# Chunked delta rule: one head per step in three streams, against two heads per step in two streams

## The chip, the core and the metric

The kernel runs on one core of a Trainium2 chip. Its time is the device time of one execution in microseconds (us). A core has TensorE (PE, whose weight loads are shown as PEld), VectorE (DVE), ScalarE (ACT), GpSimd (POOL) and SyncE (SP, which issues the transfers). Each of them works through its own instructions in the order in which the program gives them, and waits for the others through semaphores.

## The reference

Two transformer-like blocks on 256 tokens of width 1024, all in float32. The first block mixes tokens with a gated delta rule over 8 heads of 128 columns, in chunks:

```python
# per head; in the kernel a chunk is 128 rows, so 2 chunks per head
decay = exp(where(causal, g[c] - g[s], -inf))
lower = where(strict, (k_beta @ k.T) * decay, 0)
t_inv = triangular_solve(eye + lower, eye, lower=True, unit_diagonal=True)
u  = t_inv @ v_beta;  w = t_inv @ (k_beta * exp(g))
qk = where(causal, (q @ k.T) * decay, 0)
v_new = u - w @ state
o     = q_g @ state + qk @ v_new
state = state * exp(g_last) + k_dec.T @ v_new
```

Around it stand the projections (q, k, v, z, gates, a short convolution branch, `proj`, `wo`), an FFN, then a second block with attention and a gated FFN. All of them are products of the 1024-wide activations with weights that are read once from HBM.

## The kernel before

**Products.** Weights are float32, read in items of 1 MB into three buffers `raw`. A unit is half an item: ACT writes its high part `wh` (fp32r, line 1459), DVE the rest `wl` (line 1851), into five buffers in turn. PE then makes, for each 128-column tile of a unit, 12 matmuls of 128 rows by 256 columns: 8 on line 1094 (high activations with `wh` and `wl`) and 4 on line 1100 (low activations with `wh`). Such a row of 12 matmuls is a *tick* below; a product of 256 columns has 4 ticks. Ticks are counted here from the first product (q of the first two heads). Up to tick 50 come q, k, v (and the small `ab`), to 98 the three of the convolution branch, then gb to 114, z to 130, scout to 146, ga to 162, proj to 178, wo to 194. Beside gb, z and scout DVE also sums one item of the modulation weights per product (`ada`: lines 1747 and 1750, on 128x512).

**The order.** A planner in Python writes one list of events. After each tick it calls `tick()`, which lets every open task add its next event; all engines then walk the same list and take their own part of each event. So an event that falls after tick 40 stands on PE between the matmuls of ticks 40 and 41, whenever its operands come.

**The delta rule.** The task `gdn(h)` carries head `h` through 21 steps. Step `k` adds the event `gdn` (PE's part of it, in `pe_gdn`) and `gdn_out` `k+1` (what ACT, DVE and POOL make of its result, in `act_gdn`, `dve_gdn`, `pool_engine`). Three heads are open at a time, each with its own PSUM bank (5 to 7) and tiles; `beat` makes the steps fall alternately one and two ticks apart. The steps:

- 0: PE spreads the head's decay row over all partitions (lines 1113, 1114: 8 rows by 128 columns of weights, 256 columns moving) and turns `KT` (1116). DVE makes `dec` and `k0`, ACT the exponentials (1360, 1361).
- 1: PE makes k k^T and q k^T (1120, 1122). DVE makes `l2`, `qk`, `xz`, `qg` (1651 to 1660), ACT copies the diagonal 64x64 blocks out (1365).
- 2 to 12: the inverse of the two 64x64 diagonal blocks of each chunk, doubled from 1 to 64 in six levels; `xz` holds both the inverse and its transpose, and PE updates both. Step 2 turns `xz` (1128), odd steps multiply by the level's part of the lower triangle (1139), even ones by the inverse (1147 and 1150). All these are 64x64 matmuls, one in the upper and one in the lower 64 partitions. DVE subtracts (1666), ACT copies (1373), POOL cuts the levels out (2061, 2067).
- 13, 14: the remaining 64x64 block of the 128x128 inverse (1156, 1161).
- 15 to 20: values, state, output, and the sum of squares for the norm (1166 to 1184, all 128x128 or 128x256).

After it `oz` multiplies with z and splits the result for `proj`; before `proj` starts, all tasks are drained.

**Fixed waits between the parts.** The values of heads 2j and 2j+1 need the task `conv_qkv`: ACT's block of SiLU, squares and high parts (from line 1540 to 1549, with a load of the SiLU table in front), then a transpose on PE (1298) and two sums (1305, 1307), then exponentials again, for which `ln_exp` loads the other table.

Of the kernel before, what the change touches and what calls it, by code (L numbers as in the profile page):

```python
# [11 lines left out]
T = 256  # L12
# [4 lines left out]
APART = 1  # L17
LN_EXP = 6
LATER = 6
STREAMS = 3  # L20
WARM = 9
LEVELS = [1, 2, 4, 8, 16, 32]
# [14 lines left out]
for _name, _n in (("eye", 128), ("ones", 128), ("eps", 1), ("lnq", 1), ("cmask", 128), ("eye64", 64), ("lev", 6 * 64)):  # L37
    CST[_name] = _at
    _at += _n
# [4 lines left out]
def constants():  # L44
# [5 lines left out]
    s, t = i[:, None] % 64, i[None, 0:64]  # L50
    c[:, CST["eye64"]:CST["eye64"] + 64] = s == t
    for n, m in enumerate(LEVELS):
        lev = (s // (2 * m) == t // (2 * m)) & (s // m % 2 == 0) & (t // m % 2 == 1)
        c[:, CST["lev"] + 64 * n:CST["lev"] + 64 * (n + 1)] = np.where(lev, -1.0 if n == 0 else 1.0, 0.0)
# [54 lines left out]
class Counting:  # L109
# [14 lines left out]
    def transpose(self, out, in_, eye):  # L124
        return self
# [59 lines left out]
def _program(nc, a, out, ctx):  # L185
# [3 lines left out]
    def signal(name, step=1):  # L189
# [50 lines left out]
    GH = sb("GH", [8, T], F32R, where=mixer)  # L240
    GL = sb("GL", [8, T], F32R, where=mixer)
    eyeR = sb("eyeR", [8, 8], F32R, where=mixer)
# [6 lines left out]
    streams = [dict(  # L249
        dec=sb(f"dec{i}", [128, 2, 128], where=mixer), l2=sb(f"l2{i}", [128, 2, 128], where=mixer),  # L250
        qk=sb(f"qk{i}", [128, 2, 128], where=mixer), lc=sb(f"lc{i}", [128, 2, 64], where=mixer),
        d0=sb(f"d0{i}", [128, 2, 64], where=mixer), d1=sb(f"d1{i}", [128, 2, 64], where=mixer),
        xz=sb(f"xz{i}", [128, 2, 2, 64], where=mixer), y=sb(f"y{i}", [128, 2, 64], where=mixer),
        inv=sb(f"inv{i}", [128, 2, 128], where=mixer), v=sb(f"v{i}", [128, 2, 128], where=mixer),
        s1=sb(f"s1{i}", [128, 128], where=mixer),
        k0=sb(f"k0{i}", [128, 128], where=mixer), qg=sb(f"qg{i}", [128, 128], where=mixer),
        sh=sb(f"sh{i}", [128, T], F32R, where=mixer), sl=sb(f"sl{i}", [128, T], F32R, where=mixer),
        bank=psum[8 - STREAMS + i]) for i in range(STREAMS)]
# [42 lines left out]
    lev = cst[:, CST["lev"]:CST["lev"] + 384].rearrange("p (a b) -> p a b", a=6)  # L301
    eye64 = cst[:, CST["eye64"]:CST["eye64"] + 64]
    lo, hi = slice(0, 64), slice(64, 128)
    c0, c1 = slice(0, 128), slice(128, 256)
# [88 lines left out]
    main, misc = Ring(range(3)), Ring((3, 4))  # L393
# [201 lines left out]
    def conv_qkv(p):  # L595
# [33 lines left out]
        tasks.append(gdn(2 * j))  # L629
        tasks.append(gdn(2 * j + 1))  # L630
# [16 lines left out]
    before_head, before_attend = {}, {}  # L647

    def beat(k):

        yield
        while ticks[0] % 3 != (1 if k in (0, 2, 4, 6, 8, 10, 12, 14, 17) else 0):
            yield

    def gdn(h):
        while not open_streams:
            yield
        st, before_head[h] = open_streams.pop(0)
        while ("decays", 4, 0) not in made:
            yield  # L660
        if before_head[h] is None:
            for _ in range(APART * st):
                yield from beat(0)
        yield from beat(0)
        for k in range(21):
            emit("gdn", h, k, st)
            emit("gdn_out", h, k + 1, st)
            if k == 1:
                yield from beat(k)
            yield from beat(k + 1)  # L670
        open_streams.append((st, h))
        while ("z", "ready", h // 2) not in made or ("m", 3) not in made:
            yield
        while h > 1 and ("oz", h - 2, 0) not in made:
            yield
        emit("oz", h, 0)
        yield
        emit("oz", h, 1)
# [96 lines left out]
    def after(p):  # L775
# [5 lines left out]
        elif kind in ("z", "gb", "ga"):  # L781
            if kind == "ga":
                until(("gdn", 2 * j, 17), ("gdn", 2 * j + 1, 17))
# [70 lines left out]
    def operands_of(p, unit):  # L854
# [5 lines left out]
        if src == "o":  # L860
            return [("oz", kt, 1) for kt in kts]
# [1335 lines left out]
```

## Time and profile before

| | |
|---|---|
| three runs, us | 924.0, 913.3, 921.08 |
| median | 921.08 |
| the profiled execution | 913.96 |
| its span in the trace | 912.2 |
| PE busy | 881.9 us, 97% |
| DVE busy | 669.5 us, 73% |
| ACT busy | 508.0 us, 56% |
| POOL busy | 72.1 us, 8% |
| mean granted clock of TensorE | 0.998 |
| DMA | 177.31 MB, mean 194 GB/s |

Of the execution's own time, 1.8 us lie outside the span.
### The profile page before, as it was taken

The page shows a single profiled execution, that of the slowest core. Times are in us where ns is not written, and L with a number is a line of the kernel's source. Part 1 is how long each engine was busy: PE and PEld are TensorE (multiplying, and loading weights), DVE is VectorE, ACT ScalarE, POOL GpSimd, SP SyncE. Part 2 cuts the span into 40 slices and gives each one's busy share as a digit, 9 for nine tenths or more (in the row PEclk, how much of TensorE's full clock was granted, in tenths as well). Part 3 has the DMA queues.
Part 4 walks back from the last instruction along what each step waited for, and adds up shares of the span by engine and source line. Part 5 has one row for each costly group of instructions (what it writes and reads, how often), then busy time and mean ns, then how long its engine had stood idle before and what let it go on. Part 6 is the DMA issues. An engine that isn't in the chain of part 4 may idle for free.

```text
span 912.2 us, 18654 instructions
## 1 busy us (share of the span) xinstructions
PE 881.9 (97%) x8020; PEld 840.6 (92%) x8020; DVE 669.5 (73%) x1132; ACT 508.0 (56%) x822; POOL 72.1 (8%) x91
## 2 busy tenths in 40 slices
PE   5897999999999999999999999999999999999997
PEld 2797899999898989999999999999888999999997
DVE  3877877566979687677888885578666778888653
ACT  2489668453344637655354444556665567666442
POOL 0101122021001101020000000220000200000011
PEclk9999999999999999999999999999999999999999
DMA  8754232332776664465998889635332436555631
GB/s 337 277 190 170 93 137 97 139 139 97 248 259 230 233 231 164 167 216 182 269 338 292 286 291 259 227 121 189 137 141 93 182 139 210 207 185 175 251 130 47
DMA packets 27681, 177.31 MB, mean 194 GB/s; under 512 B 2864, under 2 KB 5680, under 8 KB 7504
## 3 DMA queue, kind: packets, MB, share of 16 engines
q1 hardware_dynamic: 27600, 176.13, 55.1%
q8 instruction: 63, 1.03, 0.5%
q14 instruction: 18, 0.15, 0.0%
HBM read 174.29 MB, written 1.84 MB: 193 GB/s over the span
## 4 chain that ended last, share of the span: by engine, by line
PE 76%; DVE 10%; ACT 7%; DMA 4%; issue 1%; POOL 1%; DVEq 0%; SPq 0%; ACTq 0%
PE ps L1094 42%; PE ps L1100 20%; DVE wl L1851 3%; DMA raw<-in_w_fi_dram 2%; ACT wh L1459 2%; DVE acc L1750 2%; PE ps L1092 2%; PE ps L1139 1%; PE ps L1147 1%; PE ps L1233 1%; PE ps L1150 1%; PE ps L1098 1%; DMA raw<-in_ada_dram 1%; DMA raw<-in_w_sc_dram 1%; DVE KT L1733 1%
## 5 line engine op out<-in xcount | busy, mean ns | idle before, releaser
L1851 DVE TENSOR_TENSOR wl<-raw,wh 128x1024 fp32r<-128x1024 f32 x265 | 322.0, 1235 | 76.2 <-ACT wh L1459 75.5
L1094 PE MATMUL ps<-HH,wh 128*128 128x256 f32 x1480 | 367.4, 285 | 0.7 <-ACT HH L1433 0.2
L1094 PE MATMUL ps<-HH,wl 128*128 128x256 f32 x1480 | 357.4, 278 | 0.0
L1459 ACT ACTIVATE wh<-raw 128x1024 fp32r<-128x1024 f32 x265 | 273.4, 1042 | 140.3 <-PE ps L1100 109.2
L1094 PEld LDWEIGHTS ps<-HH,wh 128*128 128x128 f32 x1480 | 279.2, 189 | 8.2 <-issue 2.9
L1094 PEld LDWEIGHTS ps<-HH,wl 128*128 128x128 f32 x1480 | 278.9, 188 | 0.4
L1100 PE MATMUL ps<-HL,wh 128*128 128x256 f32 x1480 | 226.6, 278 | 0.3 <-DVE HL L1796 0.3
L1100 PEld LDWEIGHTS ps<-HL,wh 128*128 128x128 f32 x1480 | 195.2, 188 | 0.6 <-DVE HL L1796 0.5
L1094 PE MATMUL ps<-FH,wh 128*128 128x256 f32 x352 | 84.5, 276 | 0.0
L1094 PE MATMUL ps<-FH,wl 128*128 128x256 f32 x352 | 84.5, 276 | 0.0
L1750 DVE SCALAR_TENSOR_TENSOR acc<-raw,silc,acc 128x512 f32<-128x512 f32 x101 | 76.3, 756 | 8.0 <-DMA raw<-in_ada_dram 5.0
L1094 PEld LDWEIGHTS ps<-FH,wl 128*128 128x128 f32 x352 | 66.1, 188 | 0.0
L1094 PEld LDWEIGHTS ps<-FH,wh 128*128 128x128 f32 x352 | 66.1, 188 | 0.0
L1733 DVE SCALAR_TENSOR_TENSOR tmp<-ps,vec,tmp 128x255 f32<-128x255 f32 (+2 forms) x112 | 46.1, 476 | 22.4 <-ACT tmp L1527 21.1
L1100 PE MATMUL ps<-FL,wh 128*128 128x256 f32 x352 | 55.5, 276 | 0.0
L2091 POOL TENSOR_TENSOR sq<-sq 128x256 f32<-128x256 f32 x16 | 14.8, 930 | 510.9 <-ACT sq L1501 510.7
L1100 PEld LDWEIGHTS ps<-FL,wh 128*128 128x128 f32 x352 | 47.0, 188 | 0.0
L1623 ACT ACTIVATE FH<-tmp 128x512 fp32r<-128x512 f32 x22 | 13.9, 633 | 57.7 <-DVE tmp L2019 30.1
L1094 PE MATMUL ps<-YH,wh 128*128 128x256 f32 x128 | 32.0, 286 | 0.0
L1094 PE MATMUL ps<-YH,wl 128*128 128x256 f32 x128 | 30.9, 277 | 0.0
L1094 PEld LDWEIGHTS ps<-YH,wh 128*128 128x128 f32 x128 | 24.1, 188 | 0.5
L1527 ACT ACTIVATE tmp<-ps,vec 128x256 f32<-128x256 f32 x44 | 22.1, 552 | 3.6 <-PE ps L1100 3.6
(273 smaller groups left out, 1088.2 us busy)
## 6 DMA issues: line engine op xcount, KB each, us to landing
raw<-in_ada_dram SPq DMA_DIRECT2D x32, 1024.0 KB, 5.4
raw<-in_w_fi_dram SPq DMA_DIRECT2D x22, 1024.0 KB, 5.0
raw<-in_w_up_dram SPq DMA_DIRECT2D x22, 1024.0 KB, 4.8
raw<-in_w_rest_dram SPq DMA_DIRECT2D x20, 1024.0 KB, 4.7
raw<-in_w_in_dram SPq DMA_DIRECT2D x16, 1024.0 KB, 4.8
raw<-in_w_qkv_dram SPq DMA_DIRECT2D x12, 1024.0 KB, 4.8
raw<-in_w_o_dram SPq DMA_DIRECT2D x8, 1024.0 KB, 4.9
raw<-in_w_fo_dram SPq DMA_DIRECT2D x8, 1024.0 KB, 4.9
```

The lines of the kernel that those rows point to most:

```text
L1092: e.matmul(o, x_hi[:, k0 + k, 128 * t:128 * t + 128], w[:, k, :], start=first and n + k == 0, **MM)
L1094: e.matmul(o, w[:, k, 128 * t:128 * t + 128], x_hi[:, k0 + k, :], start=first and n + k == 0, **MM)
L1098: ins = e.matmul(o, x_lo[:, k0 + k, 128 * t:128 * t + 128], wh[:, k, :], start=False, **MM)
L1100: ins = e.matmul(o, wh[:, k, 128 * t:128 * t + 128], x_lo[:, k0 + k, :], start=False, **MM)
L1139: ins = e.matmul(bank[g, 64 * c:64 * c + 64], S[f"d{n % 2}"][g, c, :], xz[g, 0, c, :], start=True, **MM)
L1459: e.activation(whl[u % HALF][0][:, 0:n], raw[i % RAW][:, c:c + n], ACT.Copy).then_inc(*a_hi.up(u))
L1527: e.activation(tmps[m][:, T * t:T * t + T], b[:, T * t:T * t + T], ACT.Identity, scale=v("conv2", 88 + ft), bias=v("conv2_b", ft)).then_in ...
L1623: e.activation(flat(dst, j), tmps[m][:, :], ACT.Copy).then_inc(*a_ev.up("hi", src, j))
L1733: e.scalar_tensor_tensor(out=cv, in0=b[:, T * t:T * t + T - s], scalar=tap, in1=cv, op0=ALU.mult, op1=ALU.add).then_inc(*v_ev.up("conv", n ...
L1750: ins = e.scalar_tensor_tensor(out=acc_, in0=w, scalar=c, in1=acc_, op0=ALU.mult, op1=ALU.add)
L1851: e.tensor_tensor(wl[:, 0:n], raw[i % RAW][:, c:c + n], wh[:, 0:n].bitcast(F32), ALU.subtract).then_inc(*v_lo.up(u))
L2091: e.tensor_tensor(sqs[s][:, 0:T], sqs[s][:, 0:T], sqs[s][:, T:2 * T], ALU.add).then_inc(*g_norm.up(*(("sum", n, j) if j else ("part", n, 0))))
```

## The change

Two heads (a *pair*, 2j and 2j+1) go through every step together, on tiles of four parts (two heads by two chunks) and one PSUM bank. Two pairs are open at a time instead of three heads, in banks 5 and 6, and bank 7 joins the small `misc` ring until proj. Steps fall on even ticks, two ticks apart, and four ticks apart after steps 0, 1, 10 and 19; so the steps of both streams fall on the same ticks.

The diagonal is inverted in 32x32 blocks with five levels instead of six; only `z` is updated by PE, and its transpose `x` comes from a DVE block transpose after each update. Steps 11 and 12 then put two 32 blocks together to 64 (both the block and its transpose), steps 13 and 14 two 64 to 128. POOL makes all levels of the lower triangle in one instruction `d` (it was five of them), also `qg` (it was on DVE), and spreads x and z into block diagonal `x64` and `inv`. `GH`, `GL` and `eyeR` get 128 rows, of which 120 are zero, so the decay matmuls of step 0 use the whole array. The transpose of `KT` for `k0` moves from step 0 to step 15, and the scaling of it from DVE to ACT. `qk` is made one step later (step 3).

```diff
-STREAMS = 3
+STREAMS = 2
+GRID = 2
+HEAVY = (0, 1, 10, 19)
-LEVELS = [1, 2, 4, 8, 16, 32]
+LEVELS = [1, 2, 4, 8, 16]
...
     def beat(k):
 
+        for _ in range(2 if k in HEAVY else 1):
+            yield
+            while ticks[0] % GRID:
+                yield
...
         elif k == 1:
-            a_gdn.wait_ge(e, "eg", h)
-            for c in range(2):
-                e.matmul(bank[:, cs[c]], KT[:, h, cs[c]], KT[:, h, cs[c]], start=True, **MM)
-            for c in range(2):
-                ins = e.matmul(bank[:, 256 + 128 * c:384 + 128 * c], KT[:, h, cs[c]], QT[:, h, cs[c]], start=True, **MM)
-            ins.then_inc(*p_gdn.up(h, 1))
+            v_misc.wait_ge(e, "l2", j, 1)
+            a_gdn.wait_ge(e, "eg", j)
+            for i, h in heads_of:
+                for c in range(2):
+                    ins = e.matmul(b4[:, 2 * i + c, :], KT[:, h, cs[c]], KT[:, h, cs[c]], start=True, **MM)
+            ins.then_inc(*p_gdn.up(j, 1))
...
-            for c in range(2):
-                for g in (lo, hi):
-                    ins = e.matmul(bank[g, 64 * c:64 * c + 64], S[f"d{n % 2}"][g, c, :], xz[g, 0, c, :], start=True,
-                                   **MM)
-            ins.then_inc(*p_gdn.up(h, k))
-        elif k < 13:
+            v_gdn.wait_ge(e, "x", j, n - 1)
+            for i in range(4):
+                for q in quarter:
+                    ins = e.matmul(bank[q, 32 * i:32 * i + 32], S["d"][q, n - 1, i, :], x[q, i, :], start=True, **MM)
+            ins.then_inc(*p_gdn.up(j, k))
+        elif k < 11:
             n = (k - 2) // 2
-            a_gdn.wait_ge(e, "y", h, n)
-            for c in range(2):
-                for g in (lo, hi) if n < 5 else (lo,):
-                    e.matmul(bank[g, 64 * c:64 * c + 64], xz[g, 1, c, :], S["y"][g, c, :], start=True, **MM)
-            for c in range(2):
-                for g in (lo, hi):
-                    ins = e.matmul(bank[g, 128 + 64 * c:192 + 64 * c], S["y"][g, c, :], xz[g, 1, c, :], start=True,
-                                   **MM)
-            ins.then_inc(*p_gdn.up(h, k))
+            a_gdn.wait_ge(e, "y", j, n)
+            for i in range(4):
+                for q in quarter:
+                    ins = e.matmul(bank[q, 128 + 32 * i:160 + 32 * i], y[q, i, :], z[q, i, :], start=True, **MM)
+            ins.then_inc(*p_gdn.up(j, k))
...
-        elif 5 <= k < 13 and k % 2:
+        elif 5 <= k < 12 and k % 2:
             n = (k - 3) // 2
-            p_gdn.wait_ge(e, h, k - 1)
-            xz4 = xz[:, :, :, :].rearrange("p a b c -> p (a b c)")
-            e.tensor_tensor(xz4, xz4, b[:, 0:T], ALU.subtract).then_inc(*v_gdn.up("xz", h, n))
+            p_gdn.wait_ge(e, j, k - 1)
+            e.tensor_tensor(z[:, :, :], z[:, :, :], by_four(S, 128), ALU.subtract).then_inc(*v_gdn.up("z", j, n))
+            v_gdn.wait_ge(e, "z", j, n)
+            e.transpose(S["x"][:, :, :].rearrange("p a b -> p (a b)"), z[:, :, :].rearrange("p a b -> p (a b)")).then_inc(
+                *v_gdn.up("x", j, n))
...
                 if k == 2:
-                    a_gdn.wait_ge(e, "lc", h)
-                    for n in (1, 2):
-                        e.tensor_tensor(S[f"d{n % 2}"][:, :, :], S["lc"][:, :, :],
-                                        lev[:, n:n + 1, :].broadcast_to([128, 2, 64]), ALU.mult).then_inc(
-                            *g_gdn.up("d", h, n))
-                elif k in (4, 6, 8):
-                    n = (k - 2) // 2
-                    p_gdn.wait_ge(e, h, k - 1)
-                    e.tensor_tensor(S[f"d{n % 2}"][:, :, :], S["lc"][:, :, :],
-                                    lev[:, n + 2:n + 3, :].broadcast_to([128, 2, 64]), ALU.mult).then_inc(
-                        *g_gdn.up("d", h, n + 2))
+                    a_gdn.wait_ge(e, "lc", j)
+                    e.tensor_tensor(S["d"][:, :, :, :], S["lc"][:, None, :, :].broadcast_to([128, 4, 4, 32]),
+                                    lev[:, 1:5, None, :].broadcast_to([128, 4, 4, 32]), ALU.mult).then_inc(
+                        *g_gdn.up("d", j))
```

On PE, before, in the inverse of the first two heads: step 4 of both heads (banks 5 and 6) after the last low matmuls of a tick and ahead of the next tick.

```order
L1100 MATMUL ps1<-HL,wh4 128x256 x4
L1147 MATMUL ps5<-y0,xz0 64x64 x4
L1150 MATMUL ps5<-xz0,y0 64x64 x4
L1147 MATMUL ps6<-y1,xz1 64x64 x4
L1150 MATMUL ps6<-xz1,y1 64x64 x4
L1094 MATMUL ps1<-HH,wh0 128x256
```

On PE, in the change, at the corresponding place: a step of the inverse of two pairs, thus of four heads.

```order
L1120 MATMUL ps0<-HL,wh3 128x256 x4
L1163 MATMUL ps5<-x0,d0 32x32 x16
L1163 MATMUL ps6<-x1,d1 32x32 x16
L1114 MATMUL ps0<-HH,wh4 128x256
L1114 MATMUL ps0<-HH,wl4 128x256
```

Where each even step had one half-array pair of matmuls for the inverse and one for its transpose, the change has 16 matmuls of 32x32 per pair of heads, and the transposes are on DVE.

On ACT, before, around the SiLU block of heads 2 and 3: the exponentials of head 0 (lines 1360, 1361) stand behind the block.

```order
L1533 ACTIVATE tmp<-ps,vec 128x256 x2
L1459 ACTIVATE wh<-raw 128x1024
L1540 ACT_TABLE_LOAD
L1540 ACTIVATE QT<-QT 128x512
L1540 ACTIVATE KT<-KT 128x512
L1540 ACTIVATE tmp<-tmp 128x512
L1544 ACTIVATE sq<-QT 128x512
L1544 ACTIVATE sq<-KT 128x512
L1549 ACTIVATE sqh<-sq 128x512 x2
L1324 ACT_TABLE_LOAD
L1360 ACTIVATE qg<-ps 128x128
L1361 ACTIVATE dec<-dec 128x256
```

In the change, the same place: the exponentials of the first pair (lines 1413, 1415) stand ahead of the block, and the load of the other table stands further behind.

```order
L1597 ACTIVATE tmp<-ps,vec 128x256 x2
L1413 ACTIVATE dec<-dec 128x512
L1415 ACTIVATE qg<-ps 128x128 x2
L1523 ACTIVATE wh<-raw 128x1024
L1604 ACT_TABLE_LOAD
L1604 ACTIVATE QT<-QT 128x512
L1604 ACTIVATE KT<-KT 128x512
L1604 ACTIVATE tmp<-tmp 128x512
L1608 ACTIVATE sq<-QT 128x512
L1608 ACTIVATE sq<-KT 128x512
L1613 ACTIVATE sqh<-sq 128x512 x2
L1523 ACTIVATE wh<-raw 128x1024
```

The block itself is the same; what moved is the pair of exponentials that PE's step 1 waits for. Counted over the whole program, TensorE leaves full-size matmuls for a part of the array and comes back 65 times in the 64x64 steps before (and 8 times for lines 1113 and 1114), and 36 times in the change. The steps of the inverse have 528 matmuls of 64x64 before; in the change they have 592 of 32x32 (lines 1163 to 1185 of it) and 32 of 64x64. The full-size matmuls of the steps are the same in number, but for step 20, where 16 of 256 columns become 8 of 512.

## Rows read from the trace of the kernel before

**Rows 1.** The page: busy time and share of the engines.

```profile
PE 881.9 (97%) x8020; PEld 840.6 (92%) x8020; DVE 669.5 (73%) x1132; ACT 508.0 (56%) x822; POOL 72.1 (8%) x91
```

**Rows 2.** Busy time by stage: length, PE, PEld, DVE, ACT, POOL, clock, DMA.

```profile
81.80:366.81 285.01, 276.20 (x2927) 260.14 (x2927) 216.95 (x402) 159.90 (x291) 37.41 (x54) 0.99 0.49 174
81.80:136.61 54.81, 49.93 (x539) 46.57 (x540) 41.72 (x87) 39.41 (x72) 10.79 (x16) 0.97 0.36 132
136.61:238.93 102.32, 102.15 (x1133) 95.57 (x1132) 72.56 (x143) 54.06 (x103) 14.48 (x21) 1.00 0.36 127
238.93:342.32 103.39, 99.63 (x1048) 93.71 (x1047) 83.82 (x143) 49.10 (x86) 8.74 (x15) 1.00 0.69 244
...
478.44:540.70 62.26, 62.26 (x546) 62.26 (x545) 52.07 (x63) 29.29 (x34) 0.00 (x0) 1.00 0.84 289
```

**Rows 3.** What PE waited for from 80 to 370 us: us, times, longest.

```profile
PE ps L1120 <- ACT qg L1360: 6.6, 4, 4.0
PE ps L1156 <- DVE inv L1672: 1.3, 1, 1.3
PE ps L1172 <- ACT s L1379: 0.7, 1, 0.7
```

**Rows 4.** PE in order of time around two visits to the 64x64 steps.

```profile
109.75 0.63 PE L1100 MATMUL ps<-HL,wh 128*128 128x256 f32 x4
110.31 0.68 PE L1139 MATMUL ps<-xz,d 64*64 64x64 f32 x16
110.92 0.38 PE L1094 MATMUL ps<-HH,wh 128*128 128x256 f32 x1
...
111.97 0.63 PE L1100 MATMUL ps<-HL,wh 128*128 128x256 f32 x4
...
113.61 0.38 PE L1094 MATMUL ps<-HH,wh 128*128 128x256 f32 x1
```

**Rows 5.** PE in order of time, 64x64 matmuls in one half only.

```profile
144.12 0.44 PE L1156 MATMUL ps<-xz,l 64*64 64x64 f32 x4
144.47 0.45 PE L1139 MATMUL ps<-xz,d 64*64 64x64 f32 x8
```

**Rows 6.** The chain that ended last: start, us, what.

```profile
721.34 2.01 PE ps L1213 x18
```

**Rows 7.** PE in order of time around the decay matmuls.

```profile
92.24 0.62 PE L1100 MATMUL ps<-HL,wh 128*128 128x256 f32 x4
...
92.79 0.38 PE L1113 MATMUL ps<-GH,eyeR 8*128 8x256 f32 x1
...
93.21 0.33 PE L1116 MATMUL ps<-cst,KT 128*128 128x128 f32 x1
```

**Rows 8.** All engines in order of time, at the end of a SiLU block.

```profile
87.28 1.28 ACT L1324 ACT_TABLE_LOAD   x1
88.57 0.28 ACT L1360 ACTIVATE qg<-ps 128x128 f32<-128x128 f32 x1
...
88.90 1.23 PE L1120 MATMUL ps<-KT 128*128 128x128 f32 x4 [4.03 <-ACT qg L1360]
```

**Rows 9.** POOL's groups from 88 to 415 us, by shape.

```profile
L2067 POOL TENSOR_TENSOR d<-lc,cst 128x128 f32<-128x128 f32 x24 | 13.2, 561 | 70.5 <-PE ps L1139 70.5
...
L2080 POOL TENSOR_TENSOR sql<-sq,sqh 128x512 fp32r<-128x512 f32 x6 | 8.1, 1376 | 30.1 <-ACT sqh L1549 30.1
```

**Rows 10.** DVE's groups from 88 to 415 us, by shape.

```profile
L1851 DVE TENSOR_TENSOR wl<-raw,wh 128x1024 fp32r<-128x1024 f32 x83 | 103.2, 1254 | 13.7 <-ACT wh L1459 13.5
L1750 DVE SCALAR_TENSOR_TENSOR acc<-raw,silc,acc 128x512 f32<-128x512 f32 x42 | 31.7, 754 | 1.3
L1666 DVE TENSOR_TENSOR xz<-xz,ps 128x256 f32<-128x256 f32 x32 | 13.0, 417 | 14.5 <-PE ps L1150 14.2
...
L1660 DVE TENSOR_TENSOR xz<-xz,cst 128x128 f32<-128x128 f32 x8 | 4.0, 498 | 0.0
...
L1655 DVE TENSOR_TENSOR xz<-lc,cst 128x128 f32<-128x128 f32 x8 | 2.3, 292 | 3.0 <-ACT lc L1365 3.0
```

More of the change, by code:

```diff
@@ L36 @@
 _at = 0
-for _name, _n in (("eye", 128), ("ones", 128), ("eps", 1), ("lnq", 1), ("cmask", 128), ("eye64", 64), ("lev", 6 * 64)):
+for _name, _n in (("eye", 128), ("ones", 128), ("eps", 1), ("lnq", 1), ("cmask", 128), ("eye32", 32), ("own", 4), ("lev", 5 * 32)):
     CST[_name] = _at
@@ L122, in matmul, with transpose @@
         return self
-    def transpose(self, out, in_, eye):
+    def transpose(self, out, in_, eye=None):
         return self
@@ L248, in _program, with stream, one @@
     dt_y, dt_abs, dt_g = (M[0:8, n, :] for n in range(3))
[L249 to L258, printed above, removed]
+    def stream(i):
+        S = {}
+        def one(name, shape, dt=F32, where=mixer):
+            S[name] = sb(f"{name}{i}", shape, dt, where=where)
+        one("dec", [128, 4, 128])
+        with ExitStack() as turn:
+            one("l2", [128, 4, 128], where=turn)
+            one("v", [128, 2, 2, 128], where=turn)
+        one("sh", [128, 512], F32R)
+        one("sl", [128, 512], F32R)
+        one("qk", [128, 4, 128])
+        one("lc", [128, 4, 32])
+        one("d", [128, 4, 4, 32])
+        one("z", [128, 4, 32])
+        one("x", [128, 4, 32])
+        one("y", [128, 4, 32])
+        one("x64", [128, 4, 64])
+        one("y64", [128, 4, 64])
+        one("inv", [128, 4, 128])
+        one("s1", [128, 2, 128])
+        one("k0", [128, 2, 128])
+        one("qg", [128, 2, 128])
+        S["bank"] = psum[5 + i]
+        return S
+    streams = [stream(i) for i in range(STREAMS)]
     mixer.close()
@@ L953, in _program @@
             drain()
+            misc.order[:] = [b for b in misc.order if b[0] != 7]
         key = p["kind"], p["j"]
@@ L1163, in pe_gdn @@
         elif k == 15:
-            v_gdn.wait_ge(e, "inv", h)
+            v_gdn.wait_ge(e, "inv", j)
             a_misc.wait_ge(e, "vturn", j)
-            e.matmul(bank[:, c0], S["inv"][:, 0, :], V[:, h, 0, :], start=True, **MM).then_inc(*p_gdn.up(h, k))
+            for i, h in heads_of:
+                e.matmul(bank[:, 128 * i:128 * i + 128], S["inv"][:, 2 * i, :], V[:, h, 0, :], start=True, **MM)
+            for i, h in heads_of:
+                ins = e.transpose(bank[:, 256 + 128 * i:384 + 128 * i], KT[:, h, c0], eye)
@@ L1167, in pe_gdn @@
+            ins.then_inc(*p_gdn.up(j, k))
         elif k == 16:
-            v_gdn.wait_ge(e, "v0", h)
-            e.matmul(bank[:, c0], S["k0"][:, :], S["v"][:, 0, :], start=True, **MM).then_inc(*p_gdn.up(h, k))
+            a_gdn.wait_ge(e, "k0", j)
+            for i in range(2):
+                ins = e.matmul(bank[:, 128 * i:128 * i + 128], S["k0"][:, i, :], S["v"][:, i, 0, :], start=True, **MM)
+            ins.then_inc(*p_gdn.up(j, k))
         elif k == 17:
-            a_gdn.wait_ge(e, "s1", h)
@@ new lines, in pe_gdn @@
+            for i in range(2):
+                ins = e.matmul(bank[:, 128 * i:128 * i + 128], S["inv"][:, 2 * i + 1, :], S["k0"][:, i, :], start=True,
+                               **MM)
+            ins.then_inc(*p_gdn.up(j, k))
+        elif k == 19:
+            v_gdn.wait_ge(e, "v1", j)
+            g_gdn.wait_ge(e, "qg", j)
+            for i in range(2):
+                e.matmul(b4[:, 2 * i, :], S["v"][:, i, 0, :], S["qk"][:, 2 * i, :], start=True, **MM)
+                e.matmul(b4[:, 2 * i + 1, :], S["s1"][:, i, :], S["qg"][:, i, :], start=True, **MM)
+                ins = e.matmul(b4[:, 2 * i + 1, :], S["v"][:, i, 1, :], S["qk"][:, 2 * i + 1, :], start=False, **MM)
+            ins.then_inc(*p_gdn.up(j, k))
@@ L1636, in dve_gdn @@
         if k == 1:
[L1637 removed]
+            p_gdn.wait_ge(e, j, 0)
             v_misc.wait_ge(e, "neg")
             d_masks.wait_ge(e, "masks")
[L1640 to L1644 removed]
```

390 lines of the change are left out of this document (221 added, 169 removed).

## The prediction

> **What bounds the kernel now.** I read the page first: PE is busy for 97% of the span, DVE 73%, ACT 56% [rows 1]. Then the stages. The delta rule runs between ticks 28 and 162, from 81.80 to 366.81 us, and in each part of that PE has least room; DVE comes nearest from 238.93 to 342.32, with 83.8 of 103.4 us [rows 2]. Then PE's waits: from 80 to 370 us it waited visibly for 8.6 us, 6.6 of them for ACT's exponentials ahead of step 1 [rows 3]. So what PE has to do there sets the time, and a microsecond less on PE is a microsecond less in the end while the others keep up.
>
> What does the delta rule cost on PE? A stage without it gives the price of a tick: 44 ticks in 62.26 us [rows 2], 1.415 us each, 0.118 per matmul. The 134 ticks of the section need 189.6 us at that price; it took 285.0. So 95.4 us are spent on the steps, on their waits and on a few other matmuls.
>
> **The change part by part.**
>
> *Visits to a part of the array.* In [rows 4] the four low matmuls start at 109.75 and would be over at 110.22; the next tick starts at 110.92. So 8 small matmuls (16 records) cost 0.70 us. At the next visit the same reckoning gives 113.61 - 112.44 = 1.17 us for 32 records. The difference, 0.47 us for 16 records, is 0.0294 per record; what remains, 0.23 us, is the price of going there and back. With 65 visits that is 15.0 us before. The change has 36, thus 8.3, and four inner switches from 32 to 64, for which I take 0.1 each: 8.7.
>
> *The small matmuls before.* The 528 matmuls leave 1056 records. 96 of them, those of line 1147 in level five and all of 1156 and 1161, stand in one half of the array alone. There four records take 0.35 us with part of the entry in it [rows 5]; I take 0.059 each, twice 0.0294, so that two halves run at the same time and one alone does not gain. 960 x 0.0294 + 96 x 0.059 = 33.9 us. With the visits: 48.9.
>
> *The small matmuls after.* No row shows 32x32. The 32 matmuls of 64x64 go from one half to the other: 64 records x 0.059 = 3.8 us. The 592 of 32x32 leave 1184 records. 512 of the matmuls stand in four quarters, 32 in two, 48 in three (their tiles differ in rows or columns), so they can form 320 sets of records that run together. What is the price of a set? A full record of 128 columns takes 2.01 / 18 = 0.112 us [rows 6], one of 64 takes 0.059. On the line through these two, 32 columns come to 0.032; if narrowing gives nothing more, it stays 0.059. I take 0.032, because halving from 128 to 64 gave nearly half: 10.2 us, with 18.9 as the upper bound. If the quarters don't run together at all, 1184 records cost 37 us at 0.032 and 70 at 0.059; these are ends of the range and rivals below. My sum after is 8.7 + 3.8 + 10.2 = 22.7, **26.2 us less**.
>
> The two halves that run together in [rows 4] have different rows of the array and write the same PSUM bank, at different partitions. The Trainium skill (TensorEngine Tiling (Array Packing), Gotcha 1: PSUM Pressure) says that different row tiles cannot access the same PSUM bank at the same time; this trace does not agree for two tiles, and by that rule the quarters, which share a bank as well, would run one by one. The same page (Instruction Overhead) gives each matmul some 60 cycles of overhead and warns against tiling a dimension that is small already; by that rule a set would stay near the 64-column price, and the sum would be that of the upper bound, 18.9 us. No row here shows a matmul this narrow.
>
> *Decay matmuls.* With 8 rows they too leave the full array: from 92.71 (four low matmuls after 92.24) to 93.21, 0.50 us per head [rows 7]. With 128 rows they cost two plain ones, 0.24. Eight heads: **2.1 us less**. Their price with zero rows can't be below the plain one, and at 0.50 nothing would be gained.
>
> *Full-size matmuls of the steps.* Their number stays; 16 moving 256 columns become 8 moving 512. Zero. `KT`'s transpose moves from step 0 to 15: zero on PE, and step 0 no longer waits for `l2` through it.
>
> *Waits.* Before: 8.6 us visible, and in 81.80 to 136.61 the mean granted clock was 0.97 [rows 2]: after the wait of 4.0 us at 88.9 [rows 8] matmuls ran for a while at the lower level, 1.2 GHz; 3% of 54.8 is 1.6 us. Together 10.2. The first wait comes from ACT: the exponentials stand behind the SiLU block and a table load, and are ready at 88.9. In the change they stand ahead of the block, and step 1 finds them there. What is late next is the sum of line 1307, which needs squares from the same block and a POOL operation of 1.38 us [rows 9]: I take 1.3 us there, since PE arrives about 4 us earlier and had no wait before. The other waits, 4.6 us in all, arise where steps are one tick apart, 1.4 us; two ticks, and four for the long steps, take most of them. Against this the answers get longer: ACT and DVE take all four parts at a time, and each update of z is followed by a transpose on DVE. No row shows one; it lies between a plain 128x128 operation from SBUF at 0.29 and a slow one at 0.50 [rows 10], I take 0.35, near the plain one. Subtract and transpose then are 0.7 us against 0.42 before, well inside two ticks of 2.8 unless the queue in front is long. POOL's `d` has four times the elements of an operation of 0.56 us [rows 9], so 1.4 to 2.2 us, with six ticks to do it in. I leave 6 us of waits: **4.2 us less**.
>
> *DVE.* Its work falls: by the shapes of [rows 10] it is a quarter less for the steps (fewer and wider instructions, `qg` and the scaling of `k0` gone, 20 transposes new). In the stage from 238.93 the groups of the steps add up to about 20 of DVE's 83.8 us, so it comes to about 79. PE's part beyond its 48 ticks there is 103.4 - 67.9 = 35.5 us; shrunk like the whole, by 32.5 of 95.4, it leaves a stage of 91.3 us. DVE would be at 87%, against 84% in the stage at 478.44, where PE never waits for it [rows 2]. That is near enough to allow **2.5 us of new waits**. DMA moved 244 GB/s there and would have to move 277; the stage at 478.44 moved 289 without making PE wait.
>
> Sum: 26.2 + 2.1 + 4.2 - 2.5 = 30.0 us. The profiled execution took 913.96 us, so **884 us** on its terms. It is at the low end of the three runs shown (913.3 to 924.0, median 921.08). A new kernel's median should lie a few microseconds above such a low run too; I take 3 of these 7 and say 887.
>
> **The rivals.**
>
> *A, late answers.* PE's steps come at fixed ticks, and DVE works its queue in order. Where an item of the modulation sums (four operations of 0.75 us) and a `wl` (1.2) stand [rows 10] ahead of z's update, the answer takes some 5 us where the ticks leave 2.8 to 3.5. For it: twelve such items fall between ticks 98 and 146, DVE at 87%. Against: PE waited there for DVE only once in this way, 1.3 us [rows 3]. Eight waits of 1.5 us instead of the 2.5 in my sum: 887 + 9.5, some 896.
>
> *B, narrow gains nothing.* A set stays at 0.059: 8.7 us more, 896.
>
> *C, quarters in turn.* The 32x32 matmuls run one by one: 27 us more at 0.032, thus 914 (no change); at 0.059, 59 more, thus 946. This is the case on the other side: against the median of 921 it decides at (34 + 10.2) / 1184 = 0.037 us per record run alone. For it: quarters are finer than anything shown, with 48 in which two share rows. Against: the halves do run together [rows 4].
>
> *D, given back.* The section gets shorter and a later stage waits for its weights or for DVE. The stages behind it keep their own work, and DMA's mean is 194 of the 289 GB/s shown. If half were lost, 902.
>
> **How the numbers follow.** My case 0.58, A 0.16, B 0.10, C 0.11 (half of it each way), D 0.05. The range has to leave out no more than 2 in 10: from 876 (waits nearly gone, low runs) to 905, which takes in A, B, D and leaves out C. One per cent, 9 us, is about what a measurement of this kernel can tell from no change. Faster by over that means below 912: my case, A, B, D, and a little of C: 0.89. Within it: 0.06. Slower by over it: 0.05.
>
> **What would show it.** Records of the 32x32 steps should start in fours within some 0.03 us, 16 matmuls costing 0.25 us and a visit 0.23 more. Ticks 28 to 162 should take about 255 us instead of 285; the ticks from 98 to 146 some 91 to 94 instead of 103. Step 1 of the first pair should find its exponentials ready, and PE should wait a little at a sum of squares. Starts of 32x32 records that are all 0.03 or 0.06 apart show C; sets 0.06 apart show B; PE waiting for DVE's x in the stage with the modulation sums shows A. The prediction is wrong if ACT, which now answers with wider copies behind the same blocks, makes every step late, or if DVE's transpose costs several times 0.35.

## The result, and the profile after

| | before | changed |
|---|---|---|
| runs beside each other, us | 913.3 to 924.0 (4) | 885.61 to 893.53 (4) |
| median, us | 921.98 | 890.86 |
| ratio | | 0.9673, 95% interval 0.9593 to 0.9753 |
| the profiled execution, us | 913.96 | 893.02 |
| ticks 28 to 162, us | 285.0 | 257.2 |

The kernel is 3.3% faster. The predicted 887 us lies 4 us under the median. On two other chips (below) the change had medians of 889.02 and 886.26 us, ratios 0.9715 and 0.9675.

First the page of the changed kernel, busy time and share of the engines, beside [rows 1]:

```profile
PE 859.3 (96%) x8204; PEld 826.7 (93%) x8204; DVE 659.5 (74%) x1079; ACT 501.3 (56%) x770; POOL 67.2 (8%) x63
```

PE is still the bound and has 22.6 us less busy time. Then its stages, to be laid beside [rows 2] (length, PE, PEld, DVE, ACT, POOL, clock, DMA): ticks 28 to 162 in one, then ticks 28 to 50, 50 to 98, 98 to 146, and everything behind tick 162.

```profile
80.57:337.74 257.17, 246.46 (x3111) 237.76 (x3110) 207.86 (x351) 153.48 (x240) 32.50 (x26) 0.99 0.54 193
80.57:133.29 52.72, 44.64 (x638) 42.19 (x636) 41.74 (x85) 40.17 (x71) 8.94 (x8) 0.97 0.37 127
133.29:228.65 95.36, 92.72 (x1257) 88.86 (x1249) 71.64 (x132) 53.10 (x89) 14.87 (x12) 0.99 0.41 143
228.65:315.12 86.47, 86.47 (x1038) 84.09 (x1033) 75.89 (x115) 47.74 (x66) 8.69 (x6) 0.99 0.76 273
...
337.74:891.20 553.46, 545.03 (x4626) 534.00 (x4624) 394.04 (x627) 298.50 (x451) 27.89 (x27) 1.00 0.56 194
```

All of the gain is in the section of the delta rule: 2.1, 7.0 and 16.9 us in the three stages shown. The last row is what an unchanged program took behind it, 553.5 us; the kernel before took 545.4 there (366.81 to 912.20). That is why the profiled executions differ by 20.9 us and the medians by 31. Two more profiles of the same kernel, below, settle it.

PE's waits in the section, beside [rows 3] (us in total, times, longest):

```profile
PE ps L1170 <- ACT y L1424: 4.0, 1, 4.0
PE ps L1163 <- DVE x L1734: 2.6, 1, 2.6
PE ps L1163 <- DVE qk L1728: 1.6, 1, 1.6
PE ps L1351 <- ACT tmp L1604: 1.4, 1, 1.4
PE ps L1360 <- POOL sql L2165: 0.6, 1, 0.6
PE ps L1147 <- ACT qg L1415: 0.5, 1, 0.5
```

They come to 10.7 us; before they were 8.6. None of the old ones is left at its size, and each new one is somewhere else.

PE in order of time around one visit to the 32x32 steps, beside [rows 4]:

```profile
106.34 0.62 PE L1120 MATMUL ps<-HL,wh 128*128 128x256 f32 x4
...
106.88 0.45 PE L1163 MATMUL ps<-x,d 32*32 32x32 f32 x32
...
107.27 0.39 PE L1114 MATMUL ps<-HH,wh 128*128 128x256 f32 x1
107.49 0.28 PE L1114 MATMUL ps<-HH,wl 128*128 128x256 f32 x1
```

The four low matmuls would be over at 106.81 (106.34 + 4 x 0.118), the next tick starts at 107.27: 16 matmuls, for two heads, cost 0.46 us with the way there and back. Before, 8 matmuls for one head cost 0.70 [rows 4]. In the single records four start 7 ns apart, one for each quarter of the array, and the next four 31.6 ns after the first: 8 such sets are 0.25 us, and the visit is the other 0.21. The last line matters too: the second matmul of the tick starts 0.22 us behind the first, where product matmuls otherwise start 0.12 us apart. That belongs to the price of a visit as well, and comes back in the part on the prediction.

### The profile page after: what moved, and what is told of

It is laid out like the page before. It is cut to its first block, busy times and chain, and to the rows that moved or that the text cites. A ratio compares the mean times of both kernels' runs of the same rounds, so it can differ in the third digit from the quotient of the medians.

```text
span 891.2 us, 18860 instructions
## 1 busy us (share of the span) xinstructions
PE 859.3 (96%) x8204; PEld 826.7 (93%) x8204; DVE 659.5 (74%) x1079; ACT 501.3 (56%) x770; POOL 67.2 (8%) x63
## 3 DMA queue, kind: packets, MB, share of 16 engines
HBM read 174.16 MB, written 1.84 MB: 197 GB/s over the span
## 4 chain that ended last, share of the span: by engine, by line
PE 82%; DVE 9%; ACT 6%; DMA 1%; issue 1%; POOL 1%; DVEq 0%; SPq 0%; ACTq 0%
PE ps L1114 47%; PE ps L1120 23%; DVE wl L1930 2%; PE ps L1112 2%; ACT wh L1523 1%; PE ps L1286 1%; DVE acc L1829 1%; PE ps L1118 1%; DMA raw<-in_ada_dram 1%; DVE KT L1812 1%; PE ps L1306 1%; PE ps L1163 1%; PE ps L1170 1%; DMA raw<-in_w_in_dram 1%; PE ps L1260 0%
## 5 line engine op out<-in xcount | busy, mean ns | idle before, releaser
L1114 PE MATMUL ps<-HH,wl 128*128 128x256 f32 x1480 | 361.2, 280 | 0.0
```

The costliest lines, as they stand in the source:

```text
L1114: e.matmul(o, w[:, k, 128 * t:128 * t + 128], x_hi[:, k0 + k, :], start=first and n + k == 0, **MM)
```

## The experiments

Four kernels ran on a first chip (kernel before: median 916.06), four on a second (915.90), four on a third (915.55). Ratios are to the kernel before on the same chip. Where a step's wait falls ahead of tick 28 in one kernel and behind it in another, I compare ticks 0 to 162.

### The quarters in turn

```diff
-            for i in range(4):
-                for q in quarter:
+            for q in quarter:
+                for i in range(4):
```

(in the odd and the even steps 3 to 10)

> The change, with the loops of steps 3 to 10 turned round: all four matmuls of one quarter, then the next quarter, so that neighbours share their tile and can't run together except where the quarter changes. Same matmuls, same results. If the gain of the 32x32 steps rests on four quarters running together, 1024 records cost 0.032 us each instead of 0.008: 16 matmuls in some 0.9 to 1.0 us instead of 0.27, in all about 22 us more than the change. If PE's time there is set by issue or by the visit (rival), the price stays and the time is that of the change within 3 us.

Measured: 896.43 us (892.5 to 898.84), ratio 0.977 (0.9721 to 0.9819). The same place as above in its trace:

```profile
109.32 0.62 PE L1120 MATMUL ps<-HL,wh 128*128 128x256 f32 x4
109.87 0.89 PE L1163 MATMUL ps<-x,d 32*32 32x32 f32 x32
110.69 0.39 PE L1114 MATMUL ps<-HH,wh 128*128 128x256 f32 x1
```

Now 32 records take 110.69 - 109.79 = 0.90 us, 0.44 more, thus 14 us in 32 such groups. I had expected 22, from 0.032 us for each record run alone; 0.90 less the visit's 0.21 is 0.022 each. The section grew by 9.9 (267.1 us), since the wait for y fell from 4.0 to 1.9 and that for x from 2.6 to 1.8. So the order of issue matters: the quarters side by side are what makes the narrow matmuls cheap. The starts in such a group are mostly 26 to 32 ns apart, with pairs 5 ns apart among them, so some records of neighbouring quarters still ran together.

### The narrow matmuls twice

```diff
-            for i in range(4):
+            for i in (0, 1, 2, 3) * 2:
                 for q in quarter:
```

> Each 32x32 matmul of the steps 3 to 10 is issued twice, with the same result: 1024 more records in 256 sets of four, and not one visit, eviction or step more. Theory 1: the steps lie on the path and cost what they issue, 256 x 31.6 ns = 8.1 us, so section ticks 28 to 162 at 265 us. Theory 2: the time of the section is set by the answers of VectorE and ScalarE, which have the rest of the beat to come; then the matmuls are partly covered where PE waits (10.7 us of waits), and the section grows by 4 us or less. Theory 3: the 7 ns spacing is of the records alone and TensorE works longer than they show; then the next product starts later, and the section grows by more than 12 us.

Measured: 901.28 us (899.7 to 904.65), ratio 0.9844 (0.982 to 0.9867); section 270.1 us, 12.7 more than the unaltered change on that chip (257.5). The waits of its section:

```profile
PE ps L1170 <- ACT y L1424: 3.1, 1, 3.1
PE ps L1170 <- issue: 2.9, 2, 1.8
PE ps L1163 <- DVE x L1734: 2.0, 1, 2.0
```

Theory 1 has the right mechanism, but sizes it too low: all groups that stand between product matmuls took 9.6 us more than in the unaltered change, idle time left out (63.8 against 54.2), where it has 8.1. A set of four takes 37 ns on the mean of the section, not the 31.6 of the group shown. The waits that PE already had covered only 1.5 us of the extra work (y 4.0 to 3.1, x 2.6 to 2.0), so theory 2 falls: these matmuls are on the path. So does theory 3, although its total fits: the next product starts 0.12 us behind the last narrow record in both kernels. The rest is new: three pauses "issue", 3.5 us (the 2.9 above and one of 0.6 on L1163), in the middle of a run of narrow records, where PE waits for nothing that the profile shows, and a fourth of 0.5 us among the low matmuls just ahead of such a run:

```profile
240.81 1.30 PE L1170 MATMUL ps<-z,y 32*32 32x32 f32 x126
243.94 0.21 PE L1170 MATMUL ps<-z,y 32*32 32x32 f32 x2 [1.84 <-issue]
```

128 records had to be issued in about a microsecond there, and two of them came 1.84 us late. Instructions are fetched by DMA (the page has a queue of kind instruction), and from 242 to 244 us the transfers of weights took 97% of the engines; but the pause of 0.56 us at 131.8 falls where no transfer ran. That PE ran out of instructions is my guess; what held them up was not tried. With the matmuls once, the section of the change shows no such pause. 9.6 - 1.5 + 4.0 is 12.1 of the 12.7 us.

### The streams on odd and even ticks

The second pair's steps go on odd ticks, the first's on even ones, so the two streams no longer share a visit.

> The change, with the second stream on odd ticks instead of the common even ones. TensorE leaves the full array 48 times instead of 36. If a visit costs 0.23 us, 2.8 us more on TensorE in ticks 28 to 162; the waits may fall or rise by some 2 us with the other places. If the common beat matters by more than the visits (rival: it also bunches the answers, or spares them), the time moves by over 5 us either way.

Measured: 893.11 us (892.36 to 895.78), ratio 0.9743 (0.9701 to 0.9786); section 265.1, 7.9 more than the change. TensorE has 84 groups of step matmuls in its order instead of 53. The 12 additional visits at 0.23 would be 2.8 us; measured without idle time, all groups between product matmuls took 1.3 us more (55.8 against 54.5), and the slow first distances behind them 2.2 more, as they are 86 instead of 62. The waits account for the rest:

```profile
PE ps L1170 <- ACT y L1424: 6.5, 1, 6.5
PE ps L1163 <- DVE qk L1728: 2.0, 2, 1.7
```

Its waits over 0.4 us, with x 1.9, v 1.6 and four smaller, come to 15.3 instead of 10.7, and there are 10.2 us at half clock instead of 6.8 (below). So the common beat is worth something, about 3.5 us by its groups and the distances behind them; how much of the remaining 4.4 us is the beat's and how much the accident of where the y copy meets the SiLU block isn't told apart.

### The decay matmuls with 8 rows

`GH`, `GL` and `eyeR` get their 8 rows back.

> The change, with GH, GL and eyeR back at 8 rows, so that the decay matmuls of step 0 use 8 rows of the array. By the rows of before each head's two matmuls cost 0.50 us instead of 0.24: 2.1 us more in all, which a timing hardly tells and the starts in the trace do. If the zero rows cost as much as they save (rival), the starts stand as far apart as with 128 rows.

One run, 885.41 us; section 257.0 us. TensorE around the first pair's decay matmuls:

```profile
77.77 0.38 PE L1139 MATMUL ps<-GH,eyeR 8*128 8x256 f32 x1
77.99 0.28 PE L1140 MATMUL ps<-GL,eyeR 8*128 8x256 f32 x1
...
78.44 0.39 PE L1114 MATMUL ps<-HH,wh 128*128 128x256 f32 x1
```

and with 128 rows in the change:

```profile
77.39 0.28 PE L1139 MATMUL ps<-GH,eyeR 128*128 128x256 f32 x1
...
77.85 0.28 PE L1114 MATMUL ps<-HH,wh 128*128 128x256 f32 x1
```

From the first to the product behind, four matmuls take 0.67 us instead of 0.46, and the way in another 0.1: 0.3 us for a pair, 1.2 in all. Two heads back to back pay it once, so of the 2.1 us that I gave to the zero rows the pairing had already taken 0.9. (The distance behind, 78.44 to 78.66, is 0.22 us here and 0.12 with 128 rows, another 0.1 for a pair.) The section doesn't show even the 1.2, and the first of the four pairs lies ahead of it. What hides the rest is the clock: PE waited 2.6 us for x here as in the change (until 228.8 us), but no half clock followed. The row of one microsecond behind that wait, here and in the second profile of the change (the last columns are POOL, the clock, the DMA share and GB/s):

```profile
230.00:231.00 1.00, 1.00 (x10) 1.00 (x10) 1.00 (x2) 0.20 (x1) 0.00 (x0) 1.00 0.87 352
```

```profile
230.00:231.00 1.00, 1.00 (x7) 1.00 (x6) 1.00 (x2) 0.00 (x0) 0.00 (x0) 0.50 0.98 418
```

That is worth some 1.6 us to this run (below), more than the edit costs it in the section.

### No long beats, and the change beside it

```diff
-HEAVY = (0, 1, 10, 19)
+HEAVY = ()
```

> The change, with no steps of four ticks: every step two ticks after the last. Step 1 then has 2.8 us in which DVE makes four dec, ACT three exponentials; step 2 after 1 and 11 after 10, 20 after 19 likewise. My theory: TensorE waits at these steps, about 1 to 2 us at each of four places in four pairs, in part at once for both streams: 8 to 15 us more than the change. Rival: the delta rule ends 8 ticks per pair earlier and nothing waits for it, while the answers are quick enough: the same time within 3 us.

Measured: 883.86 us (881.94 to 887.07), ratio 0.9635 (0.958 to 0.969). My theory of 8 to 15 us more fell. The change itself ran again on the second chip:

> The changed kernel once more, unaltered, as the measure for the others of this set: its profiled run had a tail (ticks 392 to the end) 7 us longer than the kernel before, at an unchanged program there. Theory: that is noise of one execution, so this profile has the tail of the kernel before (185.5 us from tick 392 on, it was 192.3) and a section of 257 us for ticks 28 to 162 again; time 884 to 893. Rival: the change itself lengthens the tail, and it is again near 192 us.

Measured: 889.02 us (885.27 to 895.05), ratio 0.9715 (0.9684 to 0.9746). Section 257.5 us, and 185.5 us from tick 392 on, as in the kernel before. The longer tail of the first profile was that execution's and not the change's. And on the third chip:

> The changed kernel unaltered, as the measure on this chip: section ticks 0 to 162 at 300.5 to 301 us, time 884 to 893 us.

Measured: 886.26 us (885.16 to 893.38), ratio 0.9675 (0.9635 to 0.9714); ticks 0 to 162 in 300.46 us. Beside it:

> HEAVY empty a second time, now beside the unaltered change on one chip. Theory: the steps that PE visits together fall from 53 groups to 48 and the largest wait (y, 3.97 us in tick 42) falls to 1.45 because the pairs meet the SiLU block at another step; against that stands a wait of 3.26 us for qg in tick 28. Ticks 0 to 162 took 296.5 us against 300.5, so the median lies 3 to 6 us under the unaltered change. Rival: the first look was a lucky execution, and the two are within 1.5 us.

Measured: 881.51 us (881.14 to 883.72), ratio 0.9615 (0.958 to 0.9651), 4.7 us under the change on the same chip. This is the fastest kernel of the study. Ticks 0 to 162 of both, the change first:

```profile
37.92:338.38 300.46, 288.37 (x3460) 278.48 (x3461) 243.61 (x413) 191.24 (x300) 37.33 (x30) 0.99 0.53 192
```

```profile
38.08:335.03 296.95, 286.48 (x3460) 276.28 (x3461) 244.14 (x413) 189.77 (x299) 37.92 (x30) 0.99 0.54 194
```

and what PE waited for without long beats:

```profile
PE ps L1147 <- ACT qg L1415: 3.4, 1, 3.4
PE ps L1163 <- DVE qk L1728: 2.0, 1, 2.0
PE ps L1170 <- ACT y L1424: 1.4, 1, 1.4
PE ps L1163 <- DVE x L1734: 1.2, 2, 0.6
PE ps L1222 <- DVE k L1758: 0.9, 1, 0.9
```

The long beats were there to give step 1 time, and they do: without them it waits 3.4 us for qg, with them 0.5. But they lay the y copy behind the SiLU block (4.0 us against 1.4) and x in tick 98 behind the modulation sums (2.6 against 0.6). Waits from tick 27 on come to 9.1 us against 10.7, one stretch at half clock falls away (1.6 us), and six groups fewer between the products save 0.5 us of slow distances behind them. That is 3.7 us where 3.5 were measured. The visits themselves save nothing: what falls away are groups of full-size matmuls, both kernels go to a part of the array 36 times, and without idle time the groups take 56.7 us with long beats and 56.8 without.

### A long beat at step 0 alone

> HEAVY = (0,): only the step of the decays is followed by a long beat. Theory 1: the first exponentials get one tick more, so the wait for qg at step 1 (3.26 us without long beats) is under 1 us and the rest stays as without long beats: ticks 0 to 162 at 294 us. Theory 2: the later steps move by one tick, meet the SiLU block and the convolutions elsewhere, and a wait for qk, y or x of 3 to 5 us comes in its place, as in both kernels with the SiLU block one tick later: 299 us or more.

Measured: 885.93 us (883.7 to 886.74), ratio 0.9655 (0.9622 to 0.9688); ticks 0 to 162 in 298.3 us. Its waits:

```profile
PE ps L1163 <- DVE qk L1728: 4.6, 1, 4.6
...
PE ps L1147 <- ACT qg L1415: 0.5, 1, 0.5
```

The wait for qg is gone as planned, and one of 4.6 us for qk stands in its place. Theory 2.

### The SiLU block one tick later

One more `yield` in `conv_qkv` ahead of the event `silu`, which puts the block behind the y copy that waited for it.

> The largest wait left, 3.97 us in tick 42, is for ScalarE's copy y of one pair, which stands in its queue behind the SiLU block of the next pair. Here that block is put into the queue one tick later. Theory 1: the copy goes ahead, the wait is gone and about 4 us with it (section ticks 28 to 162 at 253, time ratio to the unaltered change 0.995). Theory 2: what the block feeds (the SiLU, the sums of squares and the l2 scales of the next pair) is needed just as urgently, so the wait reappears a few ticks later and the time stays.

Measured: 894.94 us (893.8 to 896.43), ratio 0.977 (0.9752 to 0.9789), ticks 0 to 162 in 307.3 us. Theory 1 fell.

```profile
PE ps L1164 <- DVE qk L1729: 5.4, 2, 5.1
PE ps L1352 <- ACT tmp L1605: 4.2, 2, 2.4
```

Every wait of the block's own results grew (tmp 1.4 to 4.2), and PE still waits for y, 3.1 us. The same edit without long beats:

> The edit of the SiLU block together with no long beats (HEAVY empty), which alone gave a section of 249.9 us. Theory 1: the two gains are of different waits and add, section near 246 us. Theory 2: without long beats the pairs already meet the SiLU block at another step (the wait there was 1.45 us), so this adds at most 1 us to the kernel without long beats.

Measured: 894.6 us (891.29 to 901.14), ratio 0.9772 (0.9744 to 0.9799), ticks 0 to 162 in 307.6 us: worse than the kernel without long beats by 11 us, which neither theory held. The largest waits are qg 5.2 in three, qk 5.1, y 2.7, tmp 2.6.

### GpSimd's d behind the transpose

```diff
                     a_gdn.wait_ge(e, "lc", j)
+                    v_gdn.wait_ge(e, "x", j, 0)
                     e.tensor_tensor(S["d"][:, :, :, :], ...
```

> GpSimd makes d only when VectorE has made the first x of the pair. Theory: VectorE's addition z<-z,cst (128x128) takes 1.08 us because GpSimd's d runs beside it, so now it takes 0.30 to 0.50 us, with the same work in both engines; d is ready 1.3 us later, still ahead of step 3 (at least one tick, 1.4 us, behind step 2), so ticks 0 to 162 within 1 us of 300.5, with the wait for qk in tick 36 (1.57 us) shorter by up to 0.7 us if VectorE's queue is what makes it late. Rival: the addition is slow by itself (operand shapes), then it takes 1.08 us again.

Measured: 885.51 us (885.34 to 886.48), ratio 0.9656 (0.9616 to 0.9696), ticks 0 to 162 in 300.5 us. In the change, and then with the edit:

```profile
92.78 1.21 POOL L2140 TENSOR_TENSOR d<-lc,cst 128x512 f32<-128x512 f32 x1 [0.84 <-ACT lc L1420]
93.06 1.08 DVE L1721 TENSOR_TENSOR z<-z,cst 128x128 f32<-128x128 f32 x1
```

```profile
93.64 0.29 DVE L1721 TENSOR_TENSOR z<-z,cst 128x128 f32<-128x128 f32 x1
93.97 0.31 DVE L1724 STREAM_TRANSPOSE x<-z 128x128 f32<-128x128 f32 x1
...
94.43 1.10 POOL L2141 TENSOR_TENSOR d<-lc,cst 128x512 f32<-128x512 f32 x1 [1.90 <-DVE x L1724]
```

The addition goes from 1.08 to 0.29 us in all four pairs. It was GpSimd beside it that slowed it. (`d` itself took 1.20 to 1.22 us in the change and takes 1.10 to 1.94 here.) The wait for qk fell from 1.6 to 0.8 us as well. Yet the section is as long as before: PE came to the y copy 0.87 us earlier, waited there 4.0 us all the same, and the half clock lasted 6.8 us instead of 3.4 (from 112.7 to 119.5, of which 5.5 us lie behind the wait), which took it back.

## Why the prediction was right

**The bound** was read rightly: a microsecond less of PE's own work was a microsecond less in the end. Twice the narrow matmuls cost the whole of their issue time and more.

**Visits and small matmuls, -26.2, and decay matmuls, -2.1.** To check them without the waits, I added up in both traces the time from the start of a product's matmul to the start of the next one wherever step matmuls stand between, less 0.118, and took off the idle time in it: 79.2 us before, 50.3 after, 28.9 less, where I had 28.3. The parts: a visit 0.21 (taken 0.23); a set of four quarters 31.6 ns in the group shown and 37 on the mean of the section (taken 0.032, on a line through 128 and 64 columns); a 64x64 record alone 58 ns (0.059); the decay matmuls of a pair 0.46 us from 77.39 to 77.85, so 0.23 per head (0.24). These held as far as they go. But [rows 4] stop at the first matmul behind the visit. The next line of that view is:

```profile
111.14 0.28 PE L1094 MATMUL ps<-HH,wl 128*128 128x256 f32 x1
```

It starts 0.22 us behind the one of 110.92, not 0.12. At full clock such a slow distance stands behind 78 of the 85 groups between the products before and 50 of 60 after; the others end in full-size fp32r matmuls. What all these first distances take over the usual 0.115 us is 7.87 us before and 4.93 after: a gain of 2.9 us that my sum didn't have. A visit cost about 0.1 us more than my 0.23.

**Waits, -4.2, and the squeeze on DVE, +2.5.** This is the step that failed. I had 10.2 us falling to 6, and 2.5 new ones, 8.5 together; it became 10.7 us of waits and 3.4 of half clock (half of the two stretches shown last), 14.1. Other matmuls than steps and products (the sums of squares, the transposes of v) also cost 2 us more without their waits, because they lost their place beside steps: 10 such groups stand alone where 5 did. Between the products themselves the half clock took 1.2 us more than before, and the remaining distances 1.1 less (0.1150 against 0.1158 us on the mean), for which I have no cause. Counted so, the section changed by -28.9 + 2.0 + 1.9 (waits) - 2.9 (first distances) + 1.2 - 1.1 = -27.8 us, where I had -30. That the sum came so near is partly luck: waits and half clock were 5.6 us worse than I had them, and a gain that I hadn't seen stood against that. 257.2 us came out instead of 255, and the second and third profiled execution took 886.37 and 885.16 us, where I had 884. The 3 us on top for a median had no row behind them; the three medians, 890.86, 889.02 and 886.26, lie on both sides of 887. (The chance of 0.89 in the prediction is my case, A, B and D alone; no part of C is in it.)

What failed in it is the rule I used: longer beats give the answers time, so waits go. Step 1 found its exponentials almost ready (0.5 us), as I said, and a small wait came at the sum (L1360, 0.6 us, where I had 1.3) as well as 1.4 at the transpose of v, which needs the same block. But the answers are in a queue, and the SiLU block stands in it for 4.9 us. ACT in order of time in the change:

```profile
109.00 1.28 ACT L1604 ACT_TABLE_LOAD   x1
...
112.91 1.13 ACT L1613 ACTIVATE sqh<-sq 128x512 fp32r<-128x512 f32 x2
113.94 0.25 ACT L1424 ACTIVATE y<-ps 128x128 f32<-128x128 f32 x1
```

A beat of two ticks (2.8 us), as behind the step that met it, doesn't reach over it; one of four (5.7 us) would, but stands behind steps 0, 1, 10 and 19 only. Which step waits for it is decided by where the steps fall; four kernels that moved them or it (no long beats, one long beat, the block later, and later without long beats) moved the largest wait from y to qk or qg, and only the one without long beats was measurably faster.

**Rival A, late answers**, came true once, at the entry of the stage that it named:

```profile
224.04 0.49 DVE L1826 TENSOR_SCALAR acc<-raw,silc 128x512 f32<-128x512 f32 x1
224.56 2.33 DVE L1829 SCALAR_TENSOR_TENSOR acc<-raw,silc,acc 128x512 f32<-128x512 f32 x3
226.81 0.28 DVE L1732 TENSOR_TENSOR z<-z,ps 128x128 f32<-128x128 f32 x1
227.12 0.31 DVE L1734 STREAM_TRANSPOSE x<-z 128x128 f32<-128x128 f32 x1
```

Four operations of the modulation sums ahead of z's update, 2.6 us of wait, and half clock behind it. But it was one wait and not eight: from 228.65 to 315.12 PE had no visible wait at all and the stage took 86.5 us, under the 91 to 94 that I forecast, with DVE at 88% (I had 87%) and DMA at 273 GB/s (277). The squeeze was not there.

**Rival B** (narrow gains nothing) and **C** (the quarters in turn) are refuted by the starts of the records, and C's worth by its own experiment: issued one quarter after the other, the matmuls cost 0.44 us more per 32 records, 14 us in all. The rule of the Trainium skill that I weighed (TensorEngine Tiling (Array Packing), Gotcha 1: PSUM Pressure) doesn't hold here for four row tiles either: four quarters that write one PSUM bank, each at partitions of its own, start 7 ns apart. Its section Instruction Overhead would have kept a set near the 64-column price; 31.6 ns against 58 says that for float32 at 32 columns it doesn't. (It speaks of latency; what is shown here is the distance between starts.)

**Rival D** (given back later): from tick 162 on, the second and third profile of the change took 546.2 and 545.0 us, the kernel before 545.4. Nothing is given back.

**DVE's transpose**, which no row had shown, takes 0.31 us (taken 0.35), and GpSimd's `d` 1.21 (1.4 to 2.2).

## What to carry to other kernels

Count what the bounding engine issues, mode changes included, and price it by the nearest rows: that part of the sum held within 5%. Read the price of an interruption up to where the usual spacing is back, and not up to the next start: here that was another 0.1 us. A wait behind a long block in another engine's queue isn't removed by giving every step more time; moving the steps only chooses which of them meets the block, so take the beat with the fewest groups and look where the block falls. Cutting the block is the other way, which was not tried. And check a wait's whole price: the half clock behind it, where it comes, costs as much as a small wait again, and it can hide or feign a difference of 1.6 us between two kernels.

## What the runs showed of the hardware

The granted clock behind waits. From 116 to 117 us in the third profile of the change, behind the wait of 4.0 us (columns as above):

```profile
116.00:117.00 1.00, 1.00 (x7) 1.00 (x6) 0.25 (x2) 0.53 (x2) 0.75 (x1) 0.50 0.00 0
```

0.50 is the level of 1.2 GHz, and that stretch lasts from 116.0 to 119.4 us. Product matmuls start 0.213 us apart in it instead of 0.115, so 3.4 us of it cost some 1.6 us. In the 14 profiles there are 22 waits of PE of 2.5 us or more from tick 0 to 162. With all of the fourteen longest (3.1 to 6.5 us) such a stretch came, mostly of 3.4 us; it was 6.8 us with the three of 5.1 us and more, and once with one of 4.0. It began up to 1.6 us ahead of the wait's end or up to 1.3 us behind it. Of the other eight, four had one (x, 2.5 to 2.6 us, in the three profiles of the change and with `d` behind the transpose) and four had none: x at 2.6 us with the decay matmuls of 8 rows, and tmp, qg and y at 2.6, 3.0 and 2.7 us with the block later and no long beats. Of the shorter waits four had one (1.6 to 2.0 us, one of them 1.9 with the streams apart) and most had none.

VectorE's block transpose of 128x128 float32 costs what a plain operation does (0.31 against 0.29 us). Behind a group of float32 matmuls, or of such with 8 rows, the first product matmul is followed by the second 0.20 to 0.22 us later instead of 0.12 (111.14 - 110.92 before, 107.49 - 107.27 in the change, 78.66 - 78.44 with 8 rows); behind the decay matmuls with 128 rows, which are fp32r, it is 0.12 (77.97 - 77.85).

An addition of two SBUF operands on VectorE took 1.08 us beside GpSimd's `d` and ended 0.15 us after it (94.14 and 93.99 in the change); alone it took 0.29. The multiplication just ahead of it also has two SBUF operands: it started before `d` in the change and took 0.29; without long beats it started beside another GpSimd operation and was over 0.16 us after that:

```profile
91.42 1.29 POOL L2165 TENSOR_TENSOR sql<-sq,sqh 128x512 fp32r<-128x512 f32 x1
91.86 1.01 DVE L1718 TENSOR_TENSOR z<-lc,cst 128x128 f32<-128x128 f32 x1 [3.72 <-ACT lc L1420]
```

That is what the Trainium skill states (SBUF — State Buffer, Who interferes with whom): a VectorE instruction with two SBUF inputs and a GpSimd one that reads SBUF exclude each other, and the one that comes second is blocked until the first is done. The runs agree. I had costed `d` by its own length alone and missed that it also stops VectorE.

When the number of narrow records was doubled, pauses without a named cause appeared, up to 1.84 us inside a group of 128. Why is open.
